# Hybrid diffusion step: where the two prompt tiles of a head pair stand in the attention loop

## The chip, the cores and the metric

The kernel runs on one core of a Trainium2 chip. Its measure is the device time of one execution in microseconds (us), so lower is better. A core has five engines that run their own instruction streams beside each other and meet only at semaphores: PE (TensorE, matrix products and transposes), DVE (VectorE), ACT (ScalarE), POOL (GpSimd) and SP (SyncE, which here only issues DMA transfers). PE writes its results into eight PSUM banks, and DVE and ACT fetch them from there.

## The reference, cut to what matters

One layer over 1024 sample tokens and 256 prompt tokens, 1024 channels wide: norm, one combined projection, a convolution branch, attention with 8 heads of 64 channels, a merge, an output projection, and a mixture of 16 experts. The change touches only the order inside the attention. There a sample token attends to a window of sample keys with a learned bias and to 512 cached context keys in one softmax; a prompt token attends to the 256 prompt keys and nothing else:

```python
def context_attention(q, k, v):                       # prompt tokens
    s = jnp.einsum('bqhd,bkhd->bhqk', q, k).astype(jnp.float32) * (HEAD_DIM ** -0.5)
    p = jax.nn.softmax(s, axis=-1).astype(v.dtype)
    return jnp.einsum('bhqk,bkhd->bqhd', p, v)
...
    # neighbourhood_attention: sample tokens
    s_loc = jnp.einsum('brnqhd,brnlhd->brnhql', qb, kg).astype(jnp.float32) * scale + bias[None]
    s_loc = jnp.where(mask[None, None, :, None, :, :], s_loc, -jnp.inf)
    s_ctx = jnp.einsum('brnqhd,bphd->brnhqp', qb, k_ctx).astype(jnp.float32) * scale
    p = jax.nn.softmax(jnp.concatenate([s_loc, s_ctx], axis=-1), axis=-1).astype(v.dtype)
    o = (jnp.einsum('brnhql,brnlhd->brnqhd', p[..., :L], vg)
         + jnp.einsum('brnhqp,bphd->brnqhd', p[..., L:], v_ctx))
```

## The kernel before, in words

The program is written out by hand: each engine has one block of code, and the order of its instructions is the order of the Python loops. Only semaphores tie the engines together, so an engine that waits holds up all that stands behind it.

The attention works on 4 head pairs (`HP`). Within a head pair it takes tiles of 128 queries: 8 sample tiles (`BLOCKS`: 2 halves of 8 rows, 4 blocks of 16 columns) and 2 prompt tiles, `NTL` = 10 in all, and `NP` = 40 tiles over the four pairs. Tile number `g` is pair `g // 10`, place `g % 10`. `LOC[g]` says whether it is a sample tile ("local"). Before, places 0 to 7 are sample tiles and places 8 and 9 prompt tiles.

For a sample tile and each of the two heads there are 384 window scores (`scores_local`, PSUM banks 0 and 1) and 512 context scores (`scores_context`, banks 3 and 4); for a prompt tile 256 scores in banks 3 and 4 alone. What follows is the same for both: DVE adds the bias and takes the maxima (`add_bias`, L2032; `context_max`, L2038; the negated maximum, L2065), ACT takes the exponentials (`exponentials`, L1502 for the context, L1506 for the window), PE turns the weights so that keys stand on partitions (`turn_weights`, 14 transposes for a sample tile, 4 for a prompt tile, all recorded at L793), DVE and ACT copy them out of a ring of four banks (DVE L2048 for a sample tile's three pieces CA, LA, LB, ACT L1517 for CB, DVE L2045 for a prompt tile's single piece), PE multiplies them with the values (`weigh`, 28 instructions for a sample tile, 8 for a prompt tile, recorded at L790), and DVE scales the result (L2074) by the reciprocal of the sum. That reciprocal goes its own way: POOL adds the sums (L711, or L713 for a prompt tile), DVE takes the reciprocal (L2055), POOL spreads it (L715), PE turns it (the piece R, a matmul with the identity), ACT copies it (L1515). One matmul of this number format is recorded as two instructions.

The loops are software-pipelined in rounds. I call round `g` the stretch in which PE does this (L1021 to L1029):

```python
            for g in range(NP + 1):
                if g:
                    turn_weights(g - 1)
                if g + 1 < NP and LOC[g + 1]:
                    scores_local(g + 1)
                if g:
                    weigh(g - 1)
                if g + 1 < NP:
                    scores_context(g + 1)
```

In the same round DVE takes the reciprocal for tile `g-1`, the maxima of tile `g`, between them the copies of the turned weights of `g-1`, the bias of `g+1` if it is a sample tile, and the output of `g-1`; ACT takes the exponentials of `g`. `scores_context(g + 1)` waits for the context exponentials of tile `g` (semaphore `pc_ok`), since they read the banks that it writes. The piece R waits for the copy of CA, four places before it in the ring, and for POOL (`rinv_ok`).

POOL also builds the bias tables of the next head pair: `make_bias(hp + 1, i - 4)` at places `i` = 4 to 9 (L699), from a table that SP loads (`load_bias`, L504) once the six of the pair before are made. After the last round all engines wait for the end of the attention, and the merge begins (`h_hi` on ACT, L1598, then PE at L790 with 512 columns).

Of the kernel before, what the change touches and what calls it, by code (L numbers as in the profile page):

```python
# [66 lines left out]
BLOCKS = [(hf, cb) for hf in range(ROWS // QR) for cb in range(GRID_W // QC)]  # L67
KROW0 = [0, ROWS - KROWS]
BAND0 = [min(max(QC * cb - 8, 0), GRID_W - KCOLS) for cb in range(GRID_W // QC)]
KIND = [0, 1, 1, 2]  # L70
# [16 lines left out]
def backbone(nc, A, O):  # L87
    ctx = ExitStack()
    with ctx:
        def sem(name):  # L90
            return ctx.enter_context(nc.semaphore(name))
# [230 lines left out]
        s_loc, s_ctx, s_added = sem("s_loc"), sem("s_ctx"), sem("s_added")  # L322
# [36 lines left out]
        NB = len(BLOCKS)  # L359
        NTL = NB + TP // P  # L360
        NP = HP * NTL
        LOC = [g % NTL < NB for g in range(NP)]
        NLOC = sum(LOC)
        LOC0 = [sum(LOC[:g]) for g in range(NP + 1)]


        def groups(g):

            if not LOC[g]:
                return [("P", True), ("R", False)]  # L370
# [11 lines left out]
        def ring_bank(use):  # L382
            return bank[(5, 6, 7, 2)[RING_AT[use] % 4]]

        def queries(rows, g):

            hp, i = divmod(g, NTL)
            return qT[rows, hp, P * i:P * i + P]

        def window_keys(rows, g):  # L390

            hp, i = divmod(g, NTL)
            hf, cb = BLOCKS[i]
            grid = kT[rows, hp, 0:TS].rearrange("p (r c) -> p r c", c=GRID_W)
            return grid[:, KROW0[hf]:KROW0[hf] + KROWS, BAND0[cb]:BAND0[cb] + KCOLS]
# [5 lines left out]
            return t.rearrange("p (b r c) -> p b r c", r=QR, c=QC)  # L401

        def bias_unit(g):
            hf, cb = BLOCKS[g % NTL]
            return 3 * hf + KIND[cb]

        def group_done(eng, g, kind):

            i = GROUP_AT[g, kind]
            by_dve = GROUPS[i][2]  # L410
            eng.wait_ge(tg_dve if by_dve else tg_act, sum(d == by_dve for _, _, d in GROUPS[:i + 1]))

        def ring_free(eng, use):

            i = RING_AT[use] - 4
            if i >= 0:
                g, kind = RING[i]
                if kind == "O":
                    eng.wait_ge(o_done, g + 1)
                else:  # L420
                    group_done(eng, g, kind)
# [242 lines left out]
        def _(pool):  # L664
# [20 lines left out]
            def make_bias(hp, u):  # L685

                hf, kind = divmod(u, 3)
                m = (mask_early, mask_late)[hf][:, kind]
                s0, j0 = 4 - 4 * hf, 16 - 8 * kind
                if u == 0:  # L690
                    pool.wait_ge(bias_in, 16 + 256 * (hp + 1))
                if hp == 0 and u == 3:
                    pool.wait_ge(consts_in, 32)
                if hp:
                    last = max(i for i, (f, cb) in enumerate(BLOCKS) if 3 * f + KIND[cb] == u)
                    pool.wait_ge(s_added, 2 * LOC0[NTL * (hp - 1) + last] + 2)
                for h in range(2):
                    table = braw[:, h, ::-1, ::-1][:, s0:s0 + KROWS, j0:j0 + KCOLS]
                    nc.gpsimd.tensor_tensor(bias[h][u], table, m, ALU.add).then_inc(bias_ok, 1)  # L699
# [3 lines left out]
            for g in range(NP):  # L703
                hp, i = divmod(g, NTL)
                pool.wait_ge(pc_ok, 2 * g + 2)
                if LOC[g]:
                    pool.wait_ge(pl_ok, 2 * LOC0[g] + 2)
                if g >= 2:
                    group_done(pool, g - 2, "R")
                if LOC[g]:  # L710
                    nc.gpsimd.tensor_tensor(rsum[:, g % 2, :], sums[:, g % 2, :, 0], sums[:, g % 2, :, 1], ALU.add).then_inc(sum_ok, 1)  # L711
# [76 lines left out]
        def _(pe):  # L788
            def mm(out, lhsT, rhs, start, stop):
                return nc.tensor.matmul(out, lhsT, rhs, start=start, stop=stop)  # L790

            def tr(out, in_, n):
                return nc.tensor.transpose(out, in_, ident[0:n, 0:n])  # L793
# [6 lines left out]
            for k in range(KC):  # L800
                last = tr(bank[5][:, 32 * k:32 * k + TAPS], dwr[0:TAPS, P * k:P * k + P], TAPS)
# [56 lines left out]
            for j in range(8):  # L858
                whi, wlo = g_hi_at(j), gw_down[j % 2]
                for tc, (t0, n) in enumerate(TOK):  # L860
# [5 lines left out]
                    for h in range(2):  # L866
                        out, cols = bank[2 * tc + h][:, 0:n], slice(P * h, P * h + P)
                        for k in range(KD):
# [6 lines left out]
                            last = mm(out, wlo[:, k, cols], g_up[k][:, 0, t0:t0 + n], False, k == KD - 1)  # L875
# [46 lines left out]
            def scores_local(g):  # L922

                if LOC0[g]:
                    pe.wait_ge(s_added, 2 * LOC0[g])
                for h in range(2):
                    last = mm(bank[h][:, 0:KLOC], queries(HALF[h], g), window_keys(HALF[h], g), True, True)
                last.then_inc(s_loc, 1)

            def scores_context(g):  # L930

                hp = g // NTL
                if g:
                    pe.wait_ge(pc_ok, 2 * g)
                for h in range(2):
                    keys = kcT[HALF[h], hp, :] if LOC[g] else kT[HALF[h], hp, TS:T]
                    last = mm(bank[3 + h][:, 0:PAST if LOC[g] else TP], queries(HALF[h], g), keys, True, True)
                last.then_inc(s_ctx, 1)
# [24 lines left out]
            def weigh(g):  # L963

                hp, i = divmod(g, NTL)
                ring_free(pe, (g, "O"))
                out = ring_bank((g, "O"))
                if LOC[g]:
                    hf, cb = BLOCKS[i]
                    context = [(3 + b, lambda h, b=b: vc[:, b, P * hp + DH * h:P * hp + DH * h + DH]) for b in range(4)]  # L970
                    window = [(b, lambda h, b=b: vband[hp % 2][:, 4 * cb + hf + b, DH * h:DH * h + DH]) for b in range(3)]
                    parts = context + window
                else:
                    c0 = P * (hp % 2)
                    parts = [(b, lambda h, b=b: vst[hp // 2][:, NB + b, c0 + DH * h:c0 + DH * h + DH]) for b in range(2)]
                    group_done(pe, g, "P")
                for m, (b, values) in enumerate(parts):
                    for h in range(2):
                        if g == 0 and b == 3 and h == 0:
                            pe.wait_ge(vc_in, 16)  # L980
                        if i == 0 and b == 0 and h == 0:
                            pe.wait_ge(vband_in, 256 * (hp + 1))
                        if LOC[g] and b in (0, 3):
                            group_done(pe, g, "LC"[b // 3] + "AB"[h])
                        last = mm(out[HALF[h], 0:P], values(h), PT[:, h, P * b:P * b + P],
                           m == 0, m == len(parts) - 1)
                last.then_inc(vv_ready, 1)
# [3 lines left out]
            for n in range(20):  # L991
# [22 lines left out]
                for k in range(KD):  # L1014
                    if n in (0, 4, 8) and k == 0:
                        pe.wait_ge(h_dve, 20 + 2 * n)
                    last = mm(bank[V_BANK[n]][:, 0:256], hT[:, k, P * t:P * t + P], ws[jj][:, k, :], k == 0, k == KD - 1)
# [17 lines left out]
            for tc, (t0, n) in enumerate(TOK):  # L1035
                for i in range(0, 4):
                    for s in range(2):
# [11 lines left out]
                        for which in range(2):  # L1049
                            out = bank[4 * s + which][:, 0:n]  # L1050
                            for k in range(KD):
# [4 lines left out]
                                last = mm(out, w_lo, h_hi, False, k == KD - 1)  # L1056
                        if not plain:
                            pe.wait_ge(hl_ok, 24 + 12 * tc + 12)
                            for q in range(KD):
# [6 lines left out]
                                last = mm(out, w_lo, a_hi, False, q % KC == KC - 1)  # L1066
# [92 lines left out]
            for i, src in enumerate((vals, valsR, idxf, idxfR)):  # L1159
                last = tr(bank[5][:, GP * i:GP * i + SP_ROWS], src[0:SP_ROWS, :], SP_ROWS)  # L1160
            last.then_inc(kt_ready, 1)
            pe.wait_ge(topk_ok, 2)
            for i, src in enumerate((vals, idxf)):
                last = tr(bank[6][:, GP * i:GP * i + GP], src[0:GP, :], GP)
# [660 lines left out]
        def _(dve):  # L1825
# [225 lines left out]
            for g in range(NP + 1):  # L2051
                mine = [kind for kind, by_dve in groups(g - 1) if by_dve] if g else []
                if g:
                    dve.wait_ge(sum_ok, g)
                    V_.reciprocal(recip[:, (g - 1) % 2, :], rsum[:, (g - 1) % 2, :]).then_inc(recip_ok, 1)  # L2055
                if g < NP:
                    dve.wait_ge(s_ctx, g + 1)
                    context_max(g, 0)
                for kind in mine[0:1]:
                    leave_ring(g - 1, kind)  # L2060
                if g < NP:
                    context_max(g, 1)
                    dve.wait_ge(c_max, 2 * g + 2)
                    mine_at = slice(0, 2) if LOC[g] else slice(1, 2)
                    V_.tensor_reduce(nmx[:, g % 2, :], mx[:, g % 2, :, mine_at], AX_X, ALU.max, negate=True).then_inc(nmax_ok, 1)  # L2065
                for kind in mine[1:]:
                    leave_ring(g - 1, kind)
                if g + 1 < NP and LOC[g + 1]:
                    add_bias(g + 1)
                if g:  # L2070
                    dve.wait_ge(vv_ready, g)
                    out = ring_bank((g - 1, "O"))
                    group_done(dve, g - 1, "R")
                    V_.tensor_tensor(queries(slice(0, P), g - 1), out[:, 0:P], over[:, (g - 1) % 2, :], ALU.mult).then_inc(o_done, 1)  # L2074
# [388 lines left out]
```

## Time and profile before

| what | value |
|---|---|
| median of 3 runs | 2653.05 us (2651.07 to 2655.63) |
| the profiled execution | 2651.39 us |
| its span | 2649.4 us |
| PE busy | 2551.6 us, 96% of the span |
| DVE busy | 1758.0 us, 66% |
| ACT busy | 1290.1 us, 49% |
| POOL busy | 267.5 us, 10% |
| chain that ended last | PE 93%, DVE 3%, ACT 2% |
| attention, round 1 to the end of round 40 | 407.08 to 610.33 us |

Busy time says how long an engine had an instruction in work; the chain that ended last says what the end of the span hung on. A round is read in the timeline of PE from the start of its transposes (L793, 14 or 4 of them in a row) to the start of the next round's. "Idle before" in a row is time in which the engine had nothing in work, and behind the arrow stands what ended it. Rows on the timeline merge instructions of one kind, so a short wait inside such a row shows only as a longer row, and lengths are best taken from start to start.

### The profile page before, as it was taken

The page shows a single profiled execution, that of the slowest core. Times are in us where ns is not written, and L with a number is a line of the kernel's source. Part 1 is how long each engine was busy: PE and PEld are TensorE (multiplying, and loading weights), DVE is VectorE, ACT ScalarE, POOL GpSimd, SP SyncE. Part 2 cuts the span into 40 slices and gives each one's busy share as a digit, 9 for nine tenths or more (in the row PEclk, how much of TensorE's full clock was granted, in tenths as well). Part 3 has the DMA queues.
Part 4 walks back from the last instruction along what each step waited for, and adds up shares of the span by engine and source line. Part 5 has one row for each costly group of instructions (what it writes and reads, how often), then busy time and mean ns, then how long its engine had stood idle before and what let it go on. Part 6 is the DMA issues. An engine that isn't in the chain of part 4 may idle for free.

```text
span 2649.4 us, 41575 instructions
## 1 busy us (share of the span) xinstructions
PE 2551.6 (96%) x17663; PEld 1944.8 (73%) x17663; DVE 1758.0 (66%) x2082; ACT 1290.1 (49%) x1757; POOL 267.5 (10%) x226
## 2 busy tenths in 40 slices
PE   5999999999999999599999999999999999999997
PEld 4888876667878988477777777777777777777775
DVE  5699936775343344867766767667776776677767
ACT  5211235554232322445556555565555555555566
POOL 0122012220000000201011101101100110110110
PEclk9999999999999999799999999999999999999998
DMA  8531233202333742679788889879988988897995
GB/s 273 159 96 33 75 91 62 48 25 72 96 95 96 210 140 80 211 264 295 267 293 278 279 281 302 275 266 298 297 263 282 295 277 281 279 297 265 298 309 211
DMA packets 472291, 550.66 MB, mean 208 GB/s; under 512 B 30303, under 2 KB 424140, under 8 KB 472107
## 3 DMA queue, kind: packets, MB, share of 16 engines
q1 hardware_dynamic: 464330, 526.36, 61.4%
q0 software_dynamic: 7776, 21.63, 3.6%
q8 instruction: 141, 2.31, 0.4%
q14 instruction: 44, 0.35, 0.0%
HBM read 518.58 MB, written 29.38 MB: 207 GB/s over the span
## 4 chain that ended last, share of the span: by engine, by line
PE 93%; DVE 3%; ACT 2%; DMA 1%; issue 1%; SPq 0%; POOL 0%; ACTq 0%; DVEq 0%; POOLq 0%
PE bank L790 88%; PE bank L793 5%; DMA arena<-in_x_sample 0%; ACT arena L1502 0%; DVE slot_lo L2329 0%; DVE arena L2347 0%; DMA arena<-in_cache_ctx_k 0%; DMA arena<-in_w_attn_o 0%; DVE arena L1867 0%; DVE arena L2038 0%; DVE arena L2045 0%; ACT arena L1491 0%; DVE h_down L2130 0%; DVE lo_first L2325 0%; DVE arena L2237 0%
## 5 line engine op out<-in xcount | busy, mean ns | idle before, releaser
L2325 DVE TENSOR_TENSOR slot_lo<-slot,e_hi 128x2048 fp32r<-128x2048 f32 x254 | 574.6, 2289 | 161.2 <-ACT e_hi L1722 156.6
L1722 ACT ACTIVATE e_hi<-slot 128x2048 fp32r<-128x2048 f32 x256 | 480.7, 1915 | 24.8 <-PE bank L790 24.7
L790 PE MATMUL bank<-e_hi,xe_hi 128*128 128x512 f32 x1024 | 418.9, 409 | 6.0 <-DVE xe_lo L2413 6.0
L790 PE MATMUL bank<-e_hi,xe_lo 128*128 128x512 f32 x1024 | 405.4, 396 | 0.0
L790 PE MATMUL bank<-slot_lo,xe_hi 128*128 128x512 f32 x1016 | 397.4, 391 | 0.0
L790 PE MATMUL bank<-arena 128*64 128x128 f32 (+8 forms) x2470 | 329.6, 362 | 23.0 <-ACT arena L1502 6.4
L790 PE MATMUL bank<-slot,arena 128*32 128x256 f32 x6144 | 351.2, 380 | 0.0
L2329 DVE TENSOR_TENSOR slot_lo<-slot,e_hi 128x2048 fp32r<-128x2048 f32 x128 | 288.7, 2287 | 76.6 <-ACT e_hi L1724 76.6
L790 PEld LDWEIGHTS bank<-arena 128*64 128x64 f32 (+3 forms) x2470 | 223.5, 155 | 101.2 <-issue 46.7
L790 PEld LDWEIGHTS bank<-slot,arena 128*32 128x32 f32 x6144 | 189.9, 110 | 137.5 <-issue 22.0
L1724 ACT ACTIVATE e_hi<-slot 128x2048 fp32r<-128x2048 f32 x128 | 239.3, 1911 | 28.0 <-PE bank L790 28.0
L790 PEld LDWEIGHTS bank<-e_hi,xe_hi 128*128 128x128 f32 x1024 | 192.4, 188 | 73.5 <-issue 25.9
L793 PE MATMUL bank<-arena 128*128 128x128 f32 (+2 forms) x1321 | 185.3, 277 | 46.7 <-DVE arena L1867 12.7
L793 PEld LDWEIGHTS bank<-arena 128*128 128x128 f32 (+2 forms) x1321 | 154.3, 144 | 102.9 <-issue 52.7
L790 PEld LDWEIGHTS bank<-slot_lo,xe_hi 128*128 128x128 f32 x1016 | 191.0, 188 | 47.0
L790 PEld LDWEIGHTS bank<-e_hi,xe_lo 128*128 128x128 f32 x1024 | 193.0, 188 | 37.2
L1758 ACT ACTIVATE arena<-bank 128x256 f32<-128x256 f32 x128 | 49.2, 384 | 347.3 <-PE bank L790 347.2
L1958 DVE SCALAR_TENSOR_TENSOR arena<-arena 128x1310 f32<-128x1310 f32 x120 | 213.8, 1781 | 3.9
L790 PE MATMUL bank<-e_hi,hT_hi 128*128 128x512 f32 x512 | 209.4, 409 | 0.6 <-DVE slot_lo L2329 0.6
L790 PE MATMUL bank<-e_hi,hT_lo 128*128 128x512 f32 x512 | 202.4, 395 | 0.0
L790 PE MATMUL bank<-slot_lo,hT_hi 128*128 128x512 f32 x512 | 200.1, 391 | 0.0
L751 POOL DMA_INDIRECT yacc<-arena x15 | 44.2, 2947 | 1221.9 <-DVE arena L2396 1221.9
(269 smaller groups left out, 3599.6 us busy)
## 6 DMA issues: line engine op xcount, KB each, us to landing
slot<-in_w_gate_e SPq DMA_DIRECT2D x128, 1024.0 KB, 6.0
slot<-in_w_up_e SPq DMA_DIRECT2D x128, 1024.0 KB, 8.9
slot<-in_w_down_e SPq DMA_DIRECT2D x128, 1024.0 KB, 6.9
arena<-in_w_in SPq DMA_DIRECT2D x68, 512.0 KB, 5.2
arena<-in_w_ada SPq DMA_DIRECT2D x48, 512.0 KB, 7.4
arena<-in_w_conv_pw SPq DMA_DIRECT2D x24, 256.0 KB, 5.7
arena<-in_w_attn_o SPq DMA_DIRECT2D x24, 256.0 KB, 5.4
yacc<-arena SPq DMA_DIRECT2D x10, 512.0 KB, 2.6
```

The lines of the kernel that those rows point to most:

```text
L751: nc.gpsimd.indirect_dma_start(out=yacc, out_offset=bass.IndirectOffsetOnAxis(ap=sidx[:, 0:1].bitcast(U32), axis=0), in_=ye, in_offset=Non ...
L790: return nc.tensor.matmul(out, lhsT, rhs, start=start, stop=stop)
L793: return nc.tensor.transpose(out, in_, ident[0:n, 0:n])
L1722: A_(halves(e_hi[c % 2])[:, :, rows4, :], halves(slot[q])[:, :, rows4, :], ACT.Copy).then_inc(ehi_ok, 1)
L1724: A_(e_hi[c % 2][:, 8 * h:8 * h + 8, :], slot[q][:, 8 * h:8 * h + 8, :], ACT.Copy).then_inc(ehi_ok, 1)
L1758: A_(sil[:, (c - 1) % 2, :], bank[(c - 1) % 2][:, 0:256], ACT.Silu).then_inc(silu_ok, 1)
L1958: V_.scalar_tensor_tensor(out=conv[:, k, :], in0=glu[:, k, t:t + CONV_W], scalar=dw[:, k, t:t + 1], in1=conv[:, k, :], op0=ALU.mult, op1=A ...
L2325: V_.tensor_tensor(halves(lo)[:, :, rows4, :], halves(slot[q])[:, :, rows4, :], halves(e_hi[c % 2])[:, :, rows4, :].bitcast(F32), ALU.subt ...
L2329: V_.tensor_tensor(slot_lo[q][:, rows8, :], slot[q][:, rows8, :], e_hi[c % 2][:, rows8, :].bitcast(F32), ALU.subtract).then_inc(elo_ok, 1)
```

## The change

A list `TILES` says which tile stands at which place of a head pair. The prompt tiles (8 and 9) now stand at places 3 and 7, with sample tiles 0, 1, 2, then 3, 4, 5, then 6, 7 around them. All that asked for the kind or the number of a tile by its place now goes through the list. POOL's wait before it overwrites a bias table now counts the last tile of the pair before that uses it, at its new place.

```diff
@@ -359,7 +359,8 @@
-        LOC = [g % NTL < NB for g in range(NP)]
+        TILES = [0, 1, 2, 8, 3, 4, 5, 9, 6, 7]
+        LOC = [TILES[g % NTL] < NB for g in range(NP)]
...
@@ -384,12 +385,12 @@
         def queries(rows, g):
 
-            hp, i = divmod(g, NTL)
+            hp, i = g // NTL, TILES[g % NTL]
             return qT[rows, hp, P * i:P * i + P]
 
         def window_keys(rows, g):
 
-            hp, i = divmod(g, NTL)
+            hp, i = g // NTL, TILES[g % NTL]
             hf, cb = BLOCKS[i]
...
@@ -401,7 +402,7 @@
         def bias_unit(g):
-            hf, cb = BLOCKS[g % NTL]
+            hf, cb = BLOCKS[TILES[g % NTL]]
             return 3 * hf + KIND[cb]
...
@@ -692,8 +693,8 @@
                 if hp:
-                    last = max(i for i, (f, cb) in enumerate(BLOCKS) if 3 * f + KIND[cb] == u)
-                    pool.wait_ge(s_added, 2 * LOC0[NTL * (hp - 1) + last] + 2)
+                    last = max(g for g in range(NTL * (hp - 1), NTL * hp) if LOC[g] and bias_unit(g) == u)
+                    pool.wait_ge(s_added, 2 * LOC0[last] + 2)
...
@@ -966,7 +967,7 @@
                 if LOC[g]:
-                    hf, cb = BLOCKS[i]
+                    hf, cb = BLOCKS[TILES[i]]
```

No instruction is added or removed; they change places. Two places on PE show it. The first is the round that follows the one without window scores. PE before, round 8, from the last transposes of the sample tile at place 7 (128x384 are window scores, 128x512 and 128x256 the context scores of a sample and of a prompt tile, 64x128 the weighing):

```order
L793 MATMUL bank<-arena 128x128 [waits o_done,pl_ok]
L793 MATMUL bank<-arena 128x128 x2
L790 MATMUL bank<-arena 128x128 [waits rinv_ok,tg_dve,pl_ok]
L790 MATMUL bank<-arena 64x128 [waits tg_dve,tg_act]
L790 MATMUL bank<-arena 64x128 [waits tg_act]
L790 MATMUL bank<-arena 64x128 x6
L790 MATMUL bank<-arena 64x128 [waits tg_dve] x2
L790 MATMUL bank<-arena 64x128 x4
L790 MATMUL bank<-arena 128x256 [waits pc_ok]
L790 MATMUL bank<-arena 128x256
```

PE of the changed kernel at the corresponding place, round 3, from the last transposes of the sample tile at place 2:

```order
L794 MATMUL bank<-arena 128x128 [waits o_done,pl_ok]
L794 MATMUL bank<-arena 128x128 x2
L791 MATMUL bank<-arena 128x128 [waits rinv_ok,tg_dve,pl_ok]
L791 MATMUL bank<-arena 128x384 [waits s_added]
L791 MATMUL bank<-arena 128x384
L791 MATMUL bank<-arena 64x128 [waits tg_dve,tg_act]
L791 MATMUL bank<-arena 64x128 [waits tg_act]
L791 MATMUL bank<-arena 64x128 x6
L791 MATMUL bank<-arena 64x128 [waits tg_dve] x2
L791 MATMUL bank<-arena 64x128 x4
L791 MATMUL bank<-arena 128x512 [waits pc_ok]
L791 MATMUL bank<-arena 128x512
```

The window scores of a sample tile now stand in this round, and its context scores have 512 columns, since a sample tile and no second prompt tile comes next.

The second place is where a prompt tile is turned and weighed. PE before, round 9 and the start of round 10 (both turn a prompt tile):

```order
L793 MATMUL bank<-arena 128x128 [waits tg_dve,pc_ok]
L793 MATMUL bank<-arena 128x128 x3
L790 MATMUL bank<-arena 128x128 [waits rinv_ok,tg_dve,pl_ok]
L790 MATMUL bank<-arena 128x384 [waits s_added]
L790 MATMUL bank<-arena 128x384
L790 MATMUL bank<-arena 64x128 [waits tg_dve,tg_act]
L790 MATMUL bank<-arena 64x128 x3
L790 MATMUL bank<-arena 128x512 [waits pc_ok]
L790 MATMUL bank<-arena 128x512
L793 MATMUL bank<-arena 128x128 [waits o_done,pc_ok]
L793 MATMUL bank<-arena 128x128 x3
L790 MATMUL bank<-arena 128x128 [waits rinv_ok,tg_dve,pl_ok]
```

PE of the changed kernel, round 4 and the start of round 5:

```order
L794 MATMUL bank<-arena 128x128 [waits tg_dve,pc_ok]
L794 MATMUL bank<-arena 128x128 x3
L791 MATMUL bank<-arena 128x128 [waits rinv_ok,tg_dve,pl_ok]
L791 MATMUL bank<-arena 128x384 [waits s_added]
L791 MATMUL bank<-arena 128x384
L791 MATMUL bank<-arena 64x128 [waits tg_dve,tg_act]
L791 MATMUL bank<-arena 64x128 x3
L791 MATMUL bank<-arena 128x512 [waits pc_ok]
L791 MATMUL bank<-arena 128x512
L794 MATMUL bank<-arena 128x128 [waits o_done,pc_ok]
L794 MATMUL bank<-arena 128x128 x3
L794 MATMUL bank<-arena 128x128 [waits tg_dve,pc_ok]
```

The prompt tile's short round is the same row of instructions, but 14 transposes of a sample tile follow it at once, where 4 of the second prompt tile followed before. The `pc_ok` of the 128x512 row stood for the exponentials of a prompt tile in round 9 and stands for those of a sample tile in round 4.

## Rows read from the trace of the kernel before

**Rows 1.** The page, part 4: the chain that ended last

```profile
PE 93%; DVE 3%; ACT 2%; DMA 1%; issue 1%; SPq 0%; POOL 0%; ACTq 0%; DVEq 0%; POOLq 0%
```

**Rows 2.** Windows: stretch, length, engines' busy us, granted clock, DMA share, GB/s

```profile
461.33:512.84 51.51, 49.09 (x452) 34.32 (x453) 38.05 (x109) 29.82 (x90) 16.41 (x32) 1.00 0.20 37
```

**Rows 3.** Timeline of PE, rounds 7 to 12: start, us, instructions, idle before

```profile
441.22 1.75 PE L793 MATMUL bank<-arena 128*128 128x128 f32 x14
...
445.83 1.75 PE L793 MATMUL bank<-arena 128*128 128x128 f32 x14
447.74 2.90 PE L790 MATMUL bank<-arena 128*128 128x128 f32 x34 [0.16 <-issue]
...
450.58 0.66 PE L793 MATMUL bank<-arena 128*128 128x128 f32 x4
...
453.60 1.13 PE L790 MATMUL bank<-arena 64*128 64x512 f32 x4 [0.70 <-ACT arena L1502]
454.66 0.66 PE L793 MATMUL bank<-arena 128*128 128x128 f32 x4
...
458.39 1.13 PE L790 MATMUL bank<-arena 64*128 64x512 f32 x4 [1.42 <-ACT arena L1502]
459.45 1.75 PE L793 MATMUL bank<-arena 128*128 128x128 f32 x14
461.33 4.04 PE L790 MATMUL bank<-arena 128*128 128x128 f32 x38
465.31 1.75 PE L793 MATMUL bank<-arena 128*128 128x128 f32 x14
...
470.79 1.75 PE L793 MATMUL bank<-arena 128*128 128x128 f32 x14
```

**Rows 4.** Timeline of DVE in rounds 7, 8, 10, 11 and 12

```profile
443.33 1.01 DVE L2048 COPY arena<-bank 128x384 f32<-128x384 f32 x2
...
446.96 0.68 DVE L2048 COPY arena<-bank 128x512 f32<-128x512 f32 x1
...
454.77 0.69 DVE L2038 TENSOR_REDUCE arena<-bank 128x1 f32<-128x512 f32 x1 [0.78 <-PE bank L790]
...
460.55 0.68 DVE L2048 COPY arena<-bank 128x512 f32<-128x512 f32 x1
...
465.17 0.16 DVE L2055 RECIPROCAL arena<-arena 128x2 f32<-128x2 f32 x1
```

**Rows 5.** Timeline of ACT in rounds 8, 10 and 11

```profile
449.02 0.20 ACT L1502 ACTIVATION_READ_ACCUMULATOR arena<-bank,arena 128x1 f32 x1
...
458.13 0.20 ACT L1502 ACTIVATION_READ_ACCUMULATOR arena<-bank,arena 128x1 f32 x1
...
464.59 0.27 ACT L1515 ACTIVATE arena<-bank 128x128 f32<-128x128 f32 x1
```

**Rows 6.** Timeline of PE, the attention's last rounds, and the first row after it

```profile
600.38 1.75 PE L793 MATMUL bank<-arena 128*128 128x128 f32 x14
...
609.67 0.66 PE L790 MATMUL bank<-arena 128*64 128x128 f32 x8 [0.18 <-DVE arena L2045]
610.71 7.13 PE L790 MATMUL bank<-arena 128*128 128x512 f32 x16 [0.39 <-DVE arena L2074]
```

**Rows 7.** Instructions of PE by shape in round 7: count | busy us, mean ns | idle before

```profile
L790 PE MATMUL bank<-arena 64*128 64x256 f32 x4 | 0.7, 428 | 0.0
```

**Rows 8.** Timeline of SP, the load of the next pair's bias table

```profile
456.30 7.69 SPq L504 DMA_DIRECT2D arena<-rpbp  x16
```

**Rows 9.** DMA issues between 380 and 620 us: KB each, us to landing

```profile
arena<-rpbp SPq DMA_DIRECT2D x48, 48.0 KB, 2.9
```

**Rows 10.** Timeline of POOL, round 15: the first new bias table

```profile
482.09 1.97 POOL L699 TENSOR_TENSOR arena<-arena 128x384 f32<-128x384 f32 x2
```

**Rows 11.** Windows around the start of the attention, columns as in rows 2

```profile
402.00:404.00 2.00, 0.00 (x0) 0.00 (x0) 0.00 (x0) 2.00 (x8) 0.00 (x0) 1.00 0.00 0
404.00:413.86 9.86, 8.96 (x61) 5.57 (x62) 5.60 (x17) 3.85 (x13) 0.97 (x4) 0.83 0.82 222
```

## The prediction

> **What bounds the kernel now.** I read the chain that ended last first [rows 1]: 93% of it is PE, so a microsecond that PE stands still or waits inside its own queue is a microsecond of the end, and what DVE, ACT and POOL do matters only where PE waits for it. Then the windows, one head pair long [rows 2]: 51.51 us for ten rounds, of which PE has an instruction in work for 49.09. About 2.4 us per pair are open holes, and the clock is at its higher level (granted 1.00, 2.4 GHz). Then PE's timeline through one pair [rows 3], from the start of one round's transposes to the start of the next. The reader is to see that rounds are not alike:
>
> - A, a sample tile is turned and window scores are made, in steady state: 465.31 to 470.79, 5.48 us, no hole.
> - B, a sample tile is turned, the next but one is a prompt tile, so no window scores: 441.22 to 445.83, 4.61.
> - C, the same after a B: 445.83 to 450.58, 4.75.
> - D, a prompt tile is turned, and the context scores at its end wait for a prompt tile's exponentials (hole of 0.70): 450.58 to 454.66, 4.08.
> - E, a prompt tile is turned, and the context scores wait for a sample tile's exponentials (hole of 1.42): 454.66 to 459.45, 4.79.
> - F, a sample tile is turned after an E: 459.45 to 465.31, 5.86, which is 0.38 more than A for the same instructions.
>
> A pair before is five A and one of each other: 27.40 + 4.61 + 4.75 + 4.08 + 4.79 + 5.86 = 51.49, and the window says 51.51.
>
> **Why they have these lengths.** DVE, ACT and POOL start on a round when its context scores are there, at the round's start, and need a fixed time. In E DVE begins its maximum 0.11 after the round's start, at 454.77 [rows 4], ACT's second exponential ends at 458.13 + 0.20 = 458.33 [rows 5], and PE starts the next context scores at 458.39: 3.73 us, whatever PE has to do. In a sample tile's round that time lies below 14 transposes and the weighing, in a prompt tile's it does not. F pays later: DVE's reciprocal for the sample tile waits for POOL's sum and so for the last exponentials, so its copy of piece CA comes at 460.55 and lasts to 461.23 [rows 4], and the matmul R behind the 14 transposes starts at 461.33, 1.88 after the round's start instead of the 1.59 that the transposes take. B is so short that DVE and ACT fall behind it: its copies of LA and LB run from 443.33 to 444.34 [rows 4], while PE wants them some 0.4 us earlier. So the round after a B starts with DVE late: the copy of CA lasts from 446.96 to 447.64 [rows 4], and R waits until 447.74, with the hole of 0.16 [rows 3].
>
> **The change part by part.** Every round gets the kinds of its three tiles, turned, coming and next but one. With prompt tiles at places 3 and 7 the ten rounds of a pair are: 0 and 1 A; 2 B; 3 a new kind, G; 4 E; 5 F; 6 B; 7 G; 8 E; 9 F. C and D, in which two prompt tiles meet, are gone.
>
> G is what the trace does not show: a sample tile is turned after a B, and there are window scores and a sample tile's context scores. Its parts are there. The start is that of C, since all that DVE, ACT and POOL have behind and before them there is the same (a sample tile turned, a prompt tile's maxima): 445.83 to 447.74, 1.91. From R on it holds the 38 instructions that F has from R on: 461.33 to 465.31, 3.98. Sum 5.89. The bounds: not under A, 5.48, which has the same instructions without any wait; and at most C's 4.75 plus all that the 38 have over C's 34 from R on (3.98 against 450.58 - 447.74 = 2.84, so 1.14) = 5.89. I take 5.89, as C's own late copy is the nearest row. Its context scores need the prompt tile's exponentials, which in C end at 449.02 + 0.20 [rows 5], 3.4 us into the round, and G wants them only after 4.8: the hole of 0.70 that D had is covered.
>
> E after a G instead of a D: the wait at its end hangs on its own start alone, DVE is free at that start in both (in G it has the last output behind it before the context scores, as PE weighs first), the prompt tile's copy is the same, so 4.79. F follows E as before, 5.86. B follows an A or an F; round 12 is a full A behind an F and starts level with the steady state [rows 3], so B stays 4.61.
>
> A pair then is 2 x (4.61 + 5.89 + 4.79 + 5.86) + 2 x 5.48 = 42.30 + 10.96 = 53.26, against 51.49: 1.77 us more. Where from: the hole of D is saved, but there are two E, two F and two late starts behind a B instead of one each, and B's own wait is paid twice.
>
> Whole attention: rounds 0 and 1 are the same in both orders. Rounds 2 to 37 are, before, 20 A, 4 B, and 3 each of C, D, E, F; after, 6 A, 8 B, 8 G, 7 E, 7 F. The difference is -14 x 5.48 + 4 x 4.61 + 8 x 5.89 + 4 x 4.79 + 4 x 5.86 - 3 x 4.75 - 3 x 4.08 = -76.72 + 18.44 + 47.12 + 19.16 + 23.44 - 14.25 - 12.24 = +4.95 us. So round 38, which began at 600.38 [rows 6], begins at about 605.3.
>
> The tail: before, rounds 38 to 40 turn a sample tile and two prompt tiles, and end at 609.67 + 0.66 = 610.33 [rows 6], 9.95 after 600.38. After, they are an E (4.79), then tile 38 is turned while the softmax of tile 39, a sample tile now, runs with nothing beside it, then tile 39 is turned. By the offsets of round 11 from its start at 459.45: ACT ends the last exponentials and the copy of R at 464.59 + 0.27, +5.41 [rows 5]; DVE's reciprocal for the last tile starts at 465.17, +5.72 [rows 4], and is through at +5.88; its copy of CA takes 0.6 to 0.7, so R goes at about +6.5. The transposes are done by then, as weighing tile 38 is over at about +4.4. From R to the end of the weighing are C's 2.84 less the 0.7 of the prompt tile's context scores [rows 7], 2.1, and 0.16 more until the last result has drained: +8.8. Together 4.79 + 8.8 = 13.6, 3.6 more than before. What follows (ACT's `h_hi`, then the 16 matmuls from 610.71 [rows 6]) waits for just this end, so it moves one for one, and so does all that is bound by PE behind it.
>
> Sum: +4.95 + 3.6 = +8.5 us.
>
> Edits at nothing: the instructions' number and shapes are the same, and the index arithmetic is done when the program is built. POOL's tables: unit 3 is last used at place 5 and made behind place 7, unit 5 last used at place 9 and made behind it, so the new wait is over when it is reached. The one thing that comes later is the last table of a pair, since place 9 is a sample tile now: it moves from the second half of an E to some 2.3 us into a round 10, so the load that was issued at 456.30 [rows 8] comes about 2 us later; 7.69 us of issues and 2.9 to landing [rows 8, 9] end at about 469, and the first table from it is made at 482.09 [rows 10]. Thirteen microseconds hide it; without that cover POOL alone would be late first, not PE.
>
> **A rule against this.** The window around the attention's start shows a granted clock of 0.83 [rows 11]: after 2 us and more in which PE did nothing at all (402 to 404), some 3.4 us (9.86 x 0.17 x 2) ran at the lower of the two levels, 1.2 GHz. The Trainium skill, "TensorE: Matmul & The Clock Gate", section "A second HAM failure mode: psum-queue depth-cycling", says that short pauses between groups of matmuls can suffice to make the clock swing between its two levels. Here an E hole of 1.42 us with a D hole of 0.70 just ahead left the granted clock at 1.00 (the windows of a pair hold both) [rows 2], so the trace does not bear it out for these holes; by the rule the eight of them, against three before, would cost what the first rival says.
>
> **The rivals.** First, the lower clock: each of the 8 prompt rounds is followed by a stretch like that at the start. 3.4 us at half rate is 1.7 us lost, 8 times 13.6, so 8.5 + 13.6 = +22 us, about 2673. For it: there are eight E instead of three. Against it: between them PE is busier than before, not less, as prompt rounds no longer stand in a row. 4%.
>
> Second, on the other side, the waits of E and F are an effect of two prompt tiles in a row: a sample tile right before and after gives ACT and DVE the slack to be ahead, and the context scores find the exponentials ready. It would take away the hole of 1.42 in all 8 E and the 0.38 in all 8 F: 8.5 - 8 x 1.8 = -5.9 us, faster, about 2647. Its point: it decides if the 3.73 us count from something earlier than the round's start. Against it: the maximum of tile g needs its context scores, which PE makes last in the round before, in both orders. 4%.
>
> Third, the late copy behind a B does not come in G, and the tail folds better than I have it: 8 x 0.41 = 3.3 us less and up to 1 less, so +4.2, within 0.2%. For it: G's first 1.6 us are transposes in which DVE could catch up. Against it: C shows that they do not. 10%.
>
> That the order is not what is said is excluded by the order of instructions itself.
>
> **How the numbers follow.** The forecast is made against the profiled execution: 2651.39 + 8.5 = 2659.9. The median of the runs shown is 1.7 us above it, 2653.05, so a median should be 2661.5. A measurement of this kernel tells about 0.2%, 5.3 us, from no change, and 8.5 is beyond it. My forecast has 82%. The range takes G between 5.6 and 5.89 (-2.3), the tail 0.7 either way, and the 2 us by which runs of the same kernel differ: 2656.5 to 2665.5, which leaves the first and second rival and part of the third outside. Slower by over 0.2%: the forecast's 82%, less a little for noise at the bound, and the first rival's 4%, 84%. Within 0.2%: the third rival and that noise, 12%. Faster: 4%.
>
> **What would show it.** In PE's timeline of the changed kernel: rounds 2 to 5 of 4.61, 5.89, 4.79 and 5.86 us, and again for 6 to 9; no hole of 0.70 ahead of context scores any more and eight of about 1.42 (three before), each on ACT L1503; 53.3 us from one pair to the next; the first 512-column row behind the attention at about 619.2 instead of 610.71; from there on the same lengths as before. Wrong: if the holes behind prompt tiles are shorter than 1 us, if G takes less than 5.6, if the clock is under 1.00 between 414 and 618, or if the attention ends at 619 and the time is not longer by about the same.

## The result, and the profile after

The change makes the kernel slower by 7.9 us: median 2660.87 us (2659.55 to 2661.99, 10 runs) against 2652.99 us (2651.07 to 2655.63, 10 runs), a ratio of 1.0031 with a 95% interval of 1.0023 to 1.0039. Forecast were 2661.5 and a range of 2656.5 to 2665.5.

The profiled execution of the changed kernel took 2661.99 us with a span of 2659.9. PE's timeline from round 2 on answers to [rows 3]; a round again reaches from one row of transposes (L794 now, one line further down) to the next:

```profile
413.85 1.75 PE L794 MATMUL bank<-arena 128*128 128x128 f32 x14
415.43 3.10 PE L791 MATMUL bank<-arena 128*128 128x128 f32 x34
418.46 1.75 PE L794 MATMUL bank<-arena 128*128 128x128 f32 x14
420.37 4.04 PE L791 MATMUL bank<-arena 128*128 128x128 f32 x38 [0.16 <-issue]
424.34 0.66 PE L794 MATMUL bank<-arena 128*128 128x128 f32 x4
...
428.07 1.13 PE L791 MATMUL bank<-arena 64*128 64x512 f32 x4 [1.42 <-ACT arena L1503]
429.13 1.75 PE L794 MATMUL bank<-arena 128*128 128x128 f32 x14
431.02 4.04 PE L791 MATMUL bank<-arena 128*128 128x128 f32 x38
435.00 1.75 PE L794 MATMUL bank<-arena 128*128 128x128 f32 x14
```

Rounds 2 to 5 are 4.61, 5.88, 4.79 and 5.87 us long, where B, G, E and F were worked out as 4.61, 5.89, 4.79 and 5.86. The 0.70 hole is gone and the 1.42 hole comes twice per pair. The waits list of the attention (waiter, releaser: us in total, times, longest) has eight of them, 1.4 on average as at the longest; before there were six, 6.4 us in all, the 1.42 and the 0.70 in turn:

```profile
PE bank L791 <- ACT arena L1503: 11.3, 8, 1.4
```

One whole pair, between the starts of two rounds 9 (window, length, busy us of PE, PEld, DVE, ACT, POOL, granted clock, DMA share, GB/s), answers to [rows 2]:

```profile
450.28:503.54 53.26, 49.82 (x454) 34.43 (x452) 37.94 (x108) 29.81 (x91) 16.44 (x32) 1.00 0.20 36
```

53.26 us instead of 51.51, with PE's recorded busy time up only by 0.73 and the granted clock unchanged. The tail answers to [rows 6]:

```profile
605.32 0.66 PE L794 MATMUL bank<-arena 128*128 128x128 f32 x4
...
610.11 1.75 PE L794 MATMUL bank<-arena 128*128 128x128 f32 x14
...
614.47 2.12 PE L794 MATMUL bank<-arena 128*128 128x128 f32 x14
616.69 2.14 PE L791 MATMUL bank<-arena 128*128 128x128 f32 x30
619.22 7.13 PE L791 MATMUL bank<-arena 128*128 128x512 f32 x16 [0.39 <-DVE arena L2075]
```

Round 38 begins at 605.32 (forecast about 605.3) and the merge's first row at 619.22 instead of 610.71. The last R starts at 616.69, 6.58 after round 39's start; forecast was about 6.5.

Since the profiled executions differ by up to 4 us outside the attention whatever the order, I compare one length across all kernels below: from the start of round 2 to the merge's first row. It is 610.71 - 413.79 = 196.92 before and 619.22 - 413.85 = 205.37 after, +8.45 us. I call it the stage. Of these, 4.88 us are there by the start of round 38 (605.32 - 413.85 = 191.47 against 600.38 - 413.79 = 186.59), where 4.95 were worked out, and the rest comes in the tail.

### The profile page after: what moved, and what is told of

It reads as the page before. It is cut to its first block, busy times and chain, and to the rows that moved or that the text cites. A ratio compares the mean times of both kernels' runs of the same rounds, so it can differ in the third digit from the quotient of the medians.

```text
span 2659.9 us, 41575 instructions
## 1 busy us (share of the span) xinstructions
PE 2557.2 (96%) x17663; PEld 1946.7 (73%) x17663; DVE 1757.5 (66%) x2082; ACT 1290.7 (49%) x1757; POOL 266.7 (10%) x226
## 4 chain that ended last, share of the span: by engine, by line
PE 92%; DVE 3%; ACT 2%; SPq 1%; DMA 1%; issue 1%; POOL 0%; ACTq 0%; DVEq 0%; POOLq 0%
PE bank L791 87%; PE bank L794 5%; SPq L455 1%; ACT arena L1503 1%; DVE arena L2039 0%; DMA arena<-in_w_ada 0%; DVE slot_lo L2330 0%; DVE arena L2348 0%; DMA arena<-in_cache_ctx_k 0%; DMA arena<-in_w_attn_o 0%; ACT arena L1492 0%; DVE arena L2046 0%; DVE h_down L2131 0%; DVE lo_first L2326 0%; DVE arena L2238 0%
## 5 line engine op out<-in xcount | busy, mean ns | idle before, releaser
L794 PE MATMUL bank<-arena 128*128 128x128 f32 (+2 forms) x1321 | 185.4, 276 | 45.0 <-DVE arena L1868 12.2
L794 PEld LDWEIGHTS bank<-arena 128*128 128x128 f32 (+2 forms) x1321 | 153.9, 144 | 101.2 <-issue 52.7
```

## The experiments

Each is compared with the kernel before from the same set of runs, and every difference below is against it unless said otherwise. None of the kernels leaves out a part of the reference. An A round stays at 5.48 or 5.49 us in all of them.

**The changed kernel once more.**

> The changed kernel once more, on the chip and among the runs of the next three, so that they can be compared with it and not only with the kernel before. The round theory (rounds B, G, E, F twice per head pair, and a tail that ends on a sample tile) expects +8.5 us against the kernel before, all of it before the merge begins. Of its profiled execution it also tells whether the 1.7 us at about 1073 us, in which the granted clock was lower, belongs to the order: if it does, it is here again; if it is a matter of the single execution, it need not be.

Measured: 2661.12 us against 2652.74, ratio 1.0031 (1.0019 to 1.0043), +8.4. The stage is 618.88 - 413.56 = 205.32, +8.40. The lower clock behind the attention was here again. Taken alone that spoke for the order; but a kernel in the order of before has it too, in one execution of two (last section).

**Together, but in the middle of the pair.**

```diff
-        TILES = [0, 1, 2, 8, 3, 4, 5, 9, 6, 7]
+        TILES = [0, 1, 2, 3, 8, 9, 4, 5, 6, 7]
```

> The two prompt tiles stand together, at places 4 and 5 of the pair. Round theory: a period is the same as before (five A, one each of B to F, 51.49 us); rounds 2 to 37 are 2.4 us shorter than before, since the fourth pair's C to F fall into them in place of four A, and the tail is A 5.48 plus 8.4 until the end of the last sample tile, 3.9 more than before. Sum +1.5 us against the kernel before, 7 less than the changed kernel. Rival (what costs is that prompt tiles are no longer at the pair's end, by the bias tables, the loads or the place itself): as slow as the changed kernel, +8 us.

Measured: 2653.36 us, ratio 1.0003 (0.9994 to 1.0012), +0.6. Its stage is 612.74 - 414.37 = 198.37, +1.45, as worked out. PE's timeline, rounds 3 to 7:

```profile
419.85 1.75 PE L794 MATMUL bank<-arena 128*128 128x128 f32 x14
...
424.46 1.75 PE L794 MATMUL bank<-arena 128*128 128x128 f32 x14
426.38 2.91 PE L791 MATMUL bank<-arena 128*128 128x128 f32 x34 [0.16 <-issue]
429.21 0.66 PE L794 MATMUL bank<-arena 128*128 128x128 f32 x4
...
432.23 1.13 PE L791 MATMUL bank<-arena 64*128 64x512 f32 x4 [0.70 <-ACT arena L1503]
433.29 0.66 PE L794 MATMUL bank<-arena 128*128 128x128 f32 x4
...
437.02 1.13 PE L791 MATMUL bank<-arena 64*128 64x512 f32 x4 [1.42 <-ACT arena L1503]
438.08 1.75 PE L794 MATMUL bank<-arena 128*128 128x128 f32 x14
```

B, C, D and E (4.61, 4.75, 4.08, 4.79) have moved as a block to other places and kept their lengths. So the place in the pair costs nothing by itself, nor do the bias tables. Standing apart does: the changed kernel's stage is 205.37 - 198.37 = 7.00 us longer than this one's, which is four pairs at 1.77 within 0.1. The other 1.45 us go with a sample tile at the very end, which both kernels have.

**Apart, with the prompt tile's copy out of the chain.**

```diff
-                for kind in mine[0:1]:
+                behind = mine == ["P"] and g < NP
+                for kind in [] if behind else mine[0:1]:
                     leave_ring(g - 1, kind)
...
-                for kind in mine[1:]:
+                for kind in mine if behind else mine[1:]:
                     leave_ring(g - 1, kind)
```

> The changed order, but DVE copies a prompt tile's turned weights behind the second maximum and the negated maximum of the next tile, not between the two maxima. Round theory: the hole before the context scores in a prompt tile's round is set by the chain maximum, copy, maximum, negated maximum, two exponentials, counted from the round's start; without the copy in it (0.60 us) round E is 4.19 instead of 4.79, eight times: -4.8 us against the changed kernel, +3.7 against the kernel before; the eight holes are 0.8 instead of 1.42. Rival (the hole is set by ACT's or PE's own pace, or the later copy holds the weighing up as long): no change, +8 us.

Measured: 2655.92 us, ratio 1.0012 (1.0003 to 1.0021), +3.2, and 5.2 under the changed kernel of the same set. The stage is 613.09 - 412.53 = 200.56, +3.64. PE's timeline in a round E:

```profile
423.02 0.66 PE L794 MATMUL bank<-arena 128*128 128x128 f32 x4
423.52 1.23 PE L791 MATMUL bank<-arena 128*128 128x128 f32 x6
425.37 1.92 PE L791 MATMUL bank<-arena 128*64 128x128 f32 x12 [0.62 <-DVE arena L2046]
427.22 1.75 PE L794 MATMUL bank<-arena 128*128 128x128 f32 x14
```

and DVE's in the same round, with both maxima now in one row, then the negated maximum, then the copy:

```profile
423.14 1.29 DVE L2039 TENSOR_REDUCE arena<-bank 128x1 f32<-128x512 f32 x2 [0.69 <-PE bank L791]
424.46 0.16 DVE L2067 TENSOR_REDUCE arena<-arena 128x2 f32<-128x4 f32 x1
424.54 0.68 DVE L2046 COPY arena<-bank 128x512 f32<-128x512 f32 x1
```

E is 4.20 instead of 4.79: the chain from the round's start sets its length, and 0.60 of it was that copy. What I had wrong is where the hole shows. Not a shorter hole ahead of the context scores is left but one of 0.62 ahead of the weighing, which now waits for the copy; the context scores behind it sit in the same row (x12), with a wait that the row hides: from its start to the next round's are 1.85 us, where the same twelve instructions fill 1.65 in round 4 of the changed kernel (0.59 of weighing, 1.06 of context scores). ACT's second exponential ends 3.08 after the round's start, so the context scores still wait for it. The 0.62 seen and the 0.20 hidden are the 0.8 that was expected. The round's length tells, the recorded hole does not.

**Apart, with added work in the rounds that make no window scores.**

```diff
                 if g + 1 < NP and LOC[g + 1]:
                     scores_local(g + 1)
+                elif g + 1 < NP and LOC[g]:
+                    pe.wait_ge(s_added, 2 * LOC0[g + 1])
+                    for h in range(2):
+                        mm(bank[h][:, 0:KLOC], queries(HALF[h], g), window_keys(HALF[h], g), True, True)
```

> The changed order, and in each of the eight rounds that make no window scores PE makes those of the last sample tile a second time, into the same banks, where nobody reads them: 0.85 us more of PE work in each, 6.8 in all. Round theory: round B is 5.06 instead of 4.61 (its wait of 0.40 for the copies goes) and round G 5.49 instead of 5.88 (DVE no longer starts late), together 10.55 against 10.49, so the sum is +0.5 us against the changed kernel, +9 against the kernel before. Rival (B and G are bound by PE's own instructions): the added work is paid in full, +6.8 against the changed kernel, +15 against the kernel before.

Measured: 2662.09 us, ratio 1.0034 (1.0022 to 1.0047), +9.4, and 1.0 above the changed kernel of the same set, where 6.8 us of PE's work were added. The stage is 618.38 - 412.60 = 205.78, 0.41 more than the changed kernel's. PE's timeline, rounds 2 and 3:

```profile
412.60 1.75 PE L794 MATMUL bank<-arena 128*128 128x128 f32 x14
414.18 3.54 PE L791 MATMUL bank<-arena 128*128 128x128 f32 x38
417.65 1.75 PE L794 MATMUL bank<-arena 128*128 128x128 f32 x14
419.24 3.97 PE L791 MATMUL bank<-arena 128*128 128x128 f32 x38
423.14 0.66 PE L794 MATMUL bank<-arena 128*128 128x128 f32 x4
```

B is 5.05, G 5.49 and without its late R (419.24 is 1.59 behind 417.65, as long as the transposes take). The short round saves PE next to nothing: the 0.85 us that it is short of are paid for by 0.4 of waiting in it and 0.4 in the round behind it.

**The order of before, with the copy out of the chain.** The same edit as two experiments above, made in the kernel before.

> The order of the kernel before (prompt tiles together at the pair's end), but DVE copies a prompt tile's turned weights behind the second maximum and the negated maximum of the next tile. Round theory: rounds D and E of three pairs and the last pair's round 39 have the copy's 0.60 us in the chain that sets their end, seven times: -4.2 us against the kernel before. Rival (the copy is hidden, or the later weighing costs as much): no change.

Measured: 2647.01 us against 2652.26, ratio 0.998 (0.9971 to 0.9989), -5.3. The stage is 605.59 - 412.95 = 192.64, -4.28 where -4.2 was expected. D is 3.45 and E 4.19; the median's other microsecond lies outside the stage and was not traced.

**And the reciprocal behind the first maximum in F.** On top of the last one:

```diff
-                if g:
+                def reciprocals():
                     dve.wait_ge(sum_ok, g)
                     V_.reciprocal(recip[:, (g - 1) % 2, :], rsum[:, (g - 1) % 2, :]).then_inc(recip_ok, 1)
+                second = 1 < g < NP and LOC[g - 1] and not LOC[g - 2]
+                if g and not second:
+                    reciprocals()
                 if g < NP:
                     dve.wait_ge(s_ctx, g + 1)
                     context_max(g, 0)
+                if second:
+                    reciprocals()
```

> As x3, and in the round after a prompt tile's (F) DVE takes the reciprocal behind the first maximum instead of ahead of it, as the reciprocal there waits for POOL's sum and so for the last exponentials. Round theory: the copy of CA ends before the 14 transposes do, so R no longer waits, and F is 5.50 instead of 5.86, three times: -1.1 us against x3, -5.3 against the kernel before. Rival (F is late for another reason, such as POOL's spread of the reciprocal, which comes later now): no change against x3, -4.2.

Measured: 2646.57 us, ratio 0.9981 (0.9972 to 0.999), -5.7. By the medians alone, 0.4 under the kernel without it, this could not be told. The stage can: 604.70 - 413.04 = 191.66, 0.98 less, and PE's timeline has R (the x38 row) right behind the transposes at last:

```profile
457.46 1.75 PE L793 MATMUL bank<-arena 128*128 128x128 f32 x14
459.05 4.02 PE L790 MATMUL bank<-arena 128*128 128x128 f32 x38
463.01 1.20 PE L793 MATMUL bank<-arena 128*128 128x128 f32 x9
```

F is 5.55 instead of 5.86. In the kernel before, DVE's timeline has this reciprocal 0.43 after the round's start, ahead of the first maximum and the copy, and DVE idle for it:

```profile
459.88 0.17 DVE L2055 RECIPROCAL arena<-arena 128x2 f32<-128x2 f32 x1 [1.82 <-POOL arena L711]
```

So 0.31 of the 0.38 us by which F is longer than A came from DVE's order: nothing was changed in POOL's program. The other 0.07 lies inside the x38 row, which was not taken apart.

**And the owed output behind the first maximum in C.** On top of that, where `held(g)` says that round g was a B:

```diff
+            def held(g):
+                return 1 <= g and g + 1 < NP and LOC[g] and not LOC[g + 1]
...
-                second = 1 < g < NP and LOC[g - 1] and not LOC[g - 2]
+                second = 1 < g < NP and LOC[g - 1] and (not LOC[g - 2] or held(g - 1))
...
                     context_max(g, 0)
+                if held(g - 1):
+                    output(g - 2)
                 if second:
                     reciprocals()
...
-                if g:
-                    dve.wait_ge(vv_ready, g)
...
+                if g and not held(g):
+                    output(g - 1)
```

(`output(t)` holds the lines that stood under the last `if g:`. `second` now holds in this round too, so the reciprocal follows the output.)

> As x5, and in the round after a B (C) DVE takes the first maximum of the new tile ahead of the output that it still owes, and the reciprocal behind both. Round theory: C's late start is DVE waiting for ACT's copy of R of the round before; with the maximum ahead of it the copy of CA ends with the transposes, and C is 4.45 instead of 4.75, four times: -1.2 us against x5, -6.5 against the kernel before. Rival (the output, which comes no earlier, or the ring's wait for it holds PE instead): no change against x5, -5.3.

Measured: 2644.66 us, ratio 0.9971 (0.996 to 0.9981), -7.6. The stage is 603.60 - 413.26 = 190.34, -6.58 where -6.5 was expected. PE's timeline in round 8, then DVE's:

```profile
445.30 1.75 PE L793 MATMUL bank<-arena 128*128 128x128 f32 x14
446.89 2.89 PE L790 MATMUL bank<-arena 128*128 128x128 f32 x34
449.71 0.66 PE L793 MATMUL bank<-arena 128*128 128x128 f32 x4
```

```profile
445.42 0.42 DVE L2038 TENSOR_REDUCE arena<-bank 128x1 f32<-128x256 f32 x1 [1.60 <-PE bank L790]
445.83 0.29 DVE L2054 TENSOR_TENSOR arena<-bank,arena 128x128 f32<-128x128 f32 x1
446.04 0.15 DVE L2064 RECIPROCAL arena<-arena 128x2 f32<-128x2 f32 x1
446.11 0.67 DVE L2048 COPY arena<-bank 128x512 f32<-128x512 f32 x1
```

In the kernel before, DVE stands still for ACT's copy of R at this place and gives out the owed output before anything else:

```profile
446.36 0.29 DVE L2074 TENSOR_TENSOR arena<-bank,arena 128x128 f32<-128x128 f32 x1 [2.02 <-ACT arena L1515]
```

The copy of CA now starts 0.81 after the round's start instead of 446.96 - 445.83 = 1.13 [rows 3, 4], it is over when the transposes are, and C is 4.41 instead of 4.75. This version beats both kernels.

**Apart with all three, and the best once more beside it.** The changed order with the three rearrangements:

> The changed order (prompt tiles apart) with all three rearrangements of DVE's program: a prompt tile's copy behind the negated maximum, the reciprocal behind the first maximum in F, the owed output behind the first maximum in the round after a B. Round theory: E 4.19, F 5.54, G 5.88 - 0.33 = 5.55, B 4.61, each as in the runs that showed them, eight of each: -4.8 - 2.6 - 2.6 = -10 us against the changed kernel, so about 2651, no better than the kernel before, and 6.4 us above the order of before with the same three. Rival (once the late starts are gone it no longer matters where the prompt tiles stand): level with that one, about 2645.

> The order of before with the same three rearrangements, once more, on the same chip as the run beside it. Round theory and rival alike: 7.6 us under the kernel before, as measured; it is the mark that the kernel with prompt tiles apart is held against.

Measured: apart with all three 2649.65 us, ratio 0.9991 (0.9982 to 1.0001), -2.5; together with all three 2645.81, ratio 0.9975 (0.9964 to 0.9985), -6.3. The stages are 608.54 - 413.23 = 195.31 and 603.19 - 412.83 = 190.36: apart is still 4.95 longer. PE's timeline of the first:

```profile
413.23 1.75 PE L794 MATMUL bank<-arena 128*128 128x128 f32 x14
...
417.85 1.75 PE L794 MATMUL bank<-arena 128*128 128x128 f32 x14
...
423.39 0.66 PE L794 MATMUL bank<-arena 128*128 128x128 f32 x4
...
427.58 1.75 PE L794 MATMUL bank<-arena 128*128 128x128 f32 x14
...
433.13 1.75 PE L794 MATMUL bank<-arena 128*128 128x128 f32 x14
```

B, G, E, F are 4.62, 5.54, 4.19 and 5.55, so 10 us went from the changed kernel, as expected (205.37 to 195.31). The 6.4 that I had put between the two kernels was a slip: the expectations' own numbers, 8.5 - 10 = -1.5 against -6.5, give 5.0. By the medians of the two it is 3.8. The rival, that with the late starts gone the place no longer matters, is refuted: the chain in E (3.1 us of it still stand against the 2.3 us of PE's work ahead of the context scores) and the waits of B remain, and come twice per pair. A pair, from round 9 to round 19, is 50.76 us apart and 49.65 together. Four times these 1.11 us are 4.4 of the 4.95; the rest goes with the sample tile at the very end.

## Why the prediction was right

**Rounds by kind.** It priced the new order from rounds that stood in the trace, each with its neighbours: what a round costs hangs on the kinds of the tiles turned, coming and next but one, and on whether DVE starts late. All four kinds of the changed kernel came out within 0.01 us, and the together-in-the-middle kernel confirmed that they can be moved as blocks.

**G, the one kind that was not there.** C's late R (1.91) and F's 38 instructions behind it (3.98) gave 5.89; measured 5.88. The prediction put the lateness down to DVE falling behind in the short B. What holds DVE up was found only in the experiments: the output that it still owes, which waits for ACT's copy of R. With that out of the way C loses 0.34 and G 0.34, and with a longer B in front the lateness of G is gone as well.

**The hole of D, covered.** It is gone, since 4.8 us of PE's work lie ahead of the wait. That was the gain of the change, 0.7 to 0.8 us in three pairs, and it is smaller than the second E, F, B and late start.

**E and F.** E hangs on the chain that begins at its own start, shown by 0.60 us less in that chain making it 0.60 shorter in both orders (4.79 to 4.19 and 4.20). F hangs on the sum of the last exponentials by way of DVE's reciprocal, shown for 0.31 of its 0.38 us by moving that alone.

**The tail.** 13.6 us expected from round 38's start to the end of the weighing, measured 616.69 + 2.14 - 605.32 = 13.51. Together with +4.95 up to round 38 the stage was to grow by 8.5 and grew by 8.45. The two terms say where in time the cost falls and not what it is for: by the kernel with the prompt tiles in the middle, 7.0 us are the price of standing apart and 1.45 that of a sample tile at the end.

**What was not as written.** I expected the same lengths behind the attention. In the profiled execution that stretch, from the merge's first row to the span's end, took 2040.7 us instead of 2038.7, and so this execution took 2661.99 us and not 2659.9. These 2 us do not belong to the order: in the other kernels' profiled executions it is 2039.7 (the changed kernel again), 2040.6, 2038.3, 2042.7, 2039.0, 2039.8, 2038.7, 2039.5 and 2041.1. That is 2038.3 to 2042.7 with the prompt tiles apart and 2038.7 to 2041.1 with them together. 0.8 of the 2 us is a stretch at the lower clock (last section); where the rest lies was not traced. The medians, +7.9 and +8.4 us, come from several executions each. That the forecast median came within 0.6 us is closer than single runs of this kernel agree (2659.55 to 2661.99), and the upper end of the range was wider than its own terms (the tail's 0.7 and the 2 us between runs give 2664.2, not 2665.5); neither mattered here.

The first rival, a lower clock in the holes, did not happen: from round 2 to the end of the stage the granted clock is 1.00. For these holes the trace decides against the swing that the Trainium skill, "TensorE: Matmul & The Clock Gate", section "A second HAM failure mode: psum-queue depth-cycling", describes for short pauses between groups. Behind the attention a single hole of 0.72 us was followed by the lower clock in some executions (last section), so this is no finding on short pauses in general. The second rival needed the chain to begin before the context scores are there. In round 4, with a sample tile on either side, DVE still has to wait for them, and begins 0.12 after the round's start:

```profile
424.46 0.69 DVE L2039 TENSOR_REDUCE arena<-bank 128x1 f32<-128x512 f32 x1 [0.69 <-PE bank L791]
```

The third saw no late copy in G; it is there, 0.16 us of it recorded as a hole.

## What to carry to other kernels

In a software-pipelined loop over items of two kinds, where a trace of one order is at hand, write down the length of a round for each combination of neighbouring items, and price a new order as a sum of such rounds, the last rounds included. In this kernel the short items are best kept together: between long ones, each of them pays once for the long item's latency chain that it cannot cover, and once for engines that start late behind it. Where a short round waits, the cheapest cure lay not in the order of the items but in that of the engine on the chain: what the chain does not need goes behind it, and what waits for another engine goes behind what is ready; three such moves in DVE's program gave 6.3 to 7.6 us where the reordering had cost 8.

## What the runs showed of the hardware

In one place behind the attention some profiled executions ran at the lower clock, 1.2 GHz, and others did not, and the same kernel did both. The place is the same in all eleven: PE stands still for 0.72 us, waiting for ACT, then has 16 matmuls of 16 columns in 1.96 us and goes on with 512 columns. Windows of the order of before with all three rearrangements, its first profiled execution, columns as in [rows 2]:

```profile
1056.00:1060.00 4.00, 3.28 (x28) 2.46 (x21) 1.55 (x11) 1.88 (x2) 0.00 (x0) 1.00 0.54 207
1060.00:1064.00 4.00, 3.97 (x13) 2.76 (x12) 1.73 (x8) 1.75 (x3) 0.00 (x0) 0.57 0.01 2
```

and its second:

```profile
1056.00:1060.00 4.00, 3.28 (x33) 1.78 (x26) 2.15 (x11) 2.48 (x3) 0.00 (x0) 1.00 0.82 317
1060.00:1064.00 4.00, 3.40 (x20) 2.62 (x20) 1.57 (x7) 1.05 (x3) 0.00 (x0) 1.00 0.02 8
```

The lower clock came in four of the eleven: in both executions of the changed kernel (0.67 and 0.57 in the window from 1074 to 1078), in that of the apart kernel with the copy out of the chain, and in the one above. From the end of the 0.72 us to the first 512-column row on `wo_attn`, the same instructions took 6.68 to 6.88 us in these four and 5.90 to 5.92 in the other seven, so it costs 0.8 to 1.0 us. (Further on, where PE has little to do, all eleven run at the lower clock for 30 to 40 us; that stretch is not meant here.)

It is not what made the change slow: it lies outside the stage, the kernel with filled rounds does not have it and was slower still, and the apart kernel with the copy out of the chain has it and the shortest rest of all (2038.3 us). Both orders have executions with it and without, so the order alone does not decide it. What does was not tested.
